# Last expert of a layer: the down product runs bank by bank, and the output rows of the first bank are taken during the second

## What is computed

```python
def expert_choice_ffn(h, w_router, w_gate, w_up, w_down):
    ...
    aff = jax.nn.softmax(jnp.dot(xs, w_router).astype(jnp.float32), axis=-1)
    cap = EC_FACTOR * n // N_EXPERTS
    gates, idx = lax.top_k(aff.T, cap)
    xe = xs[idx]
    hid = jax.nn.silu(jnp.einsum('ecd,edf->ecf', xe, w_gate)) * jnp.einsum('ecd,edf->ecf', xe, w_up)
    ye = jnp.einsum('ecf,efd->ecd', hid, w_down) * gates[..., None].astype(h.dtype)
    out = jnp.zeros_like(xs).at[idx.reshape(-1)].add(ye.reshape(-1, D))
```

## Time and profile before

| what | us |
|---|---|
| median of 3 runs | 1947.42 |
| lowest and highest run | 1946.61, 1949.61 |
| the profiled execution, its own time | 1943.12 |
| its span | 1941.4 |
| PE busy | 1824.8 (94%) |
| DVE busy | 651.0 (34%) |
| last `down` of layer 0, first to last start | 963.61 to 975.61 |
| last `down` of layer 1, first to last start | 1914.46 to 1926.72 |

### The profile page before, as it was taken

One profiled execution on the slowest core, in us unless ns is written; L12 is line 12 of the kernel. 1 busy time (PEld: TensorE's weight loads), 2 busy tenths in 40 slices (PEclk: granted clock), 3 DMA queues, 4 the chain that ended last, 5 costly groups with the idle time before them and its releaser, 6 DMA issues. The chain is left out here.

```text
span 1941.4 us, 34715 instructions
## 1 busy us (share of the span) xinstructions
PE 1824.8 (94%) x14950; PEld 871.9 (45%) x14950; DVE 651.0 (34%) x1394; ACT 378.1 (19%) x904; POOL 200.8 (10%) x275
## 2 busy tenths in 40 slices
PE   5999989959999999999999999999599999999996
PEld 2455655422434343434455566554233434343443
DVE  2345885350212121212243457833421212121211
ACT  2224653120101000000032256421110100000000
POOL 1004300000000000000010331000000000000000
PEclk8999999979999999999999999999799999999998
DMA  9750022237999999999995201131489999999993
GB/s 385 292 227 1 1 106 114 82 137 285 389 401 399 401 405 400 411 395 412 397 356 195 109 1 65 42 152 65 179 331 396 404 400 410 398 411 394 410 387 104
DMA packets 56202, 526.51 MB, mean 271 GB/s; under 512 B 12047, under 2 KB 13695, under 8 KB 26143
## 3 DMA queue, kind: packets, MB, share of 16 engines
q1 hardware_dynamic: 49134, 501.44, 64.0%
q0 software_dynamic: 6336, 21.63, 4.7%
q10 hardware_dynamic: 672, 2.62, 0.3%
HBM read 503.91 MB, written 24.38 MB: 272 GB/s over the span
## 5 line engine op out<-in xcount | busy, mean ns | idle before, releaser
L621 PE MATMUL PS<-arena,xe 128*32 128x512 f32 x6144 | 670.2, 596 | 3.8 <-DVE xe L1438 3.8
L621 PEld LDWEIGHTS PS<-arena,xe 128*32 128x32 f32 x6144 | 195.5, 110 | 455.4 <-issue 451.1
L1449 DVE TENSOR_TENSOR RA<-RA,PS 96x512 f32<-96x512 f32 (+2 forms) x96 | 63.2, 684 | 646.9 <-ACT RA L1141 644.1
L645 PE MATMUL PS<-arena,hdT 128*32 128x512 f32 x1536 | 267.2, 596 | 6.7 <-DMA arena<-w_exp 4.8
L647 PE MATMUL PS<-arena,hdT 128*32 128x256 f32 x1024 | 264.8, 381 | 0.0
L687 PE MATMUL PS<-arena,RB 128*128 128x512 f32 (+1 forms) x480 | 183.4, 530 | 0.0
L650 PE MATMUL PS<-arena,hdT 128*32 128x256 f32 x1536 | 156.5, 380 | 0.0
L651 PE MATMUL PS<-arena,hdT 128*32 128x256 f32 x512 | 152.9, 380 | 0.0
L1141 ACT ACTIVATE RA<-PS 96x512 f32<-96x512 f32 x32 | 19.0, 593 | 670.1 <-PE PS L621 670.1
L1029 PE MATMUL PS<-arena,RB 128*128 128x512 f32 x320 | 138.9, 593 | 0.0
L647 PEld LDWEIGHTS PS<-arena,hdT 128*32 128x32 f32 x1024 | 110.2, 110 | 27.4 <-issue 0.5
(11 more groups left out here) (293 smaller groups left out, 1813.3 us busy)
## 6 DMA issues: line engine op xcount, KB each, us to landing
arena<-w_exp SPq DMA_DIRECT2D x192, 2048.0 KB, 13.4
arena<-ada_rest SPq DMA_DIRECT2D x16, 2048.0 KB, 8.2
ada<-ada_first SPq DMA_DIRECT2D x8, 2048.0 KB, 23.3
arena<-w_in SPq DMA_DIRECT2D x4, 2048.0 KB, 10.8
arena<-w_out SPq DMA_DIRECT2D x2, 4096.0 KB, 13.5
arena<-w_in SPq DMA_DIRECT2D x4, 1536.0 KB, 23.8
RC<-x_res SPq DMA_DIRECT2D x2, 2560.0 KB, 10.7
x_res<-RC SPq DMA_DIRECT2D x10, 512.0 KB, 2.6
```

The costliest lines, as they stand in the source:

```text
L621: last = mm(PS[GRP * q:GRP * (q + 1), c * 512:(c + 1) * 512], xe[:, k, GRP * grp:GRP * (grp + 1)], w[:, col_, :], start=(k == 0), stop=(k ...
L645: mm(PS[GRP * q:GRP * (q + 1), 1536:2048], tok(q), w[:, 0:512], start=first, **flags)
L1449: V.tensor_tensor(h_, h_, up, ALU.mult).then_inc(hm_rdy.sem, 1)
```

## The change

`last_down(l)` takes the place of the last `down` of each layer. It makes two sweeps over the eight chunks. The first does all that writes bank 3 and raises a new semaphore, `dn_low`; the second does all that writes bank 4. The products are the same ones, in another order. The wait for the second half of the weights stands at chunk 4 of the first sweep. `dn_used` is raised in the second sweep. On DVE `last_rows_out(l)` takes the place of the last `rows_out`: it takes 512 columns and two of the three small pieces behind `dn_low`, and 256 columns and the third small piece behind `dn_used`.

```diff
--- before.py
+++ after.py
@@ -358,6 +358,7 @@
         dn_used = Signal("dn_used", 2 * EXP, primed=True)
         sg_rdy = Signal("sg_rdy", 3 * EXP)
         hm_rdy = Signal("hm_rdy", 3 * EXP)
+        dn_low = Signal("dn_low", 1)
         ht_ps = Signal("ht_ps", EXP)
         hd_rdy = Signal("hd_rdy", EXP)
         ys_rdy = Signal("ys_rdy", EXP, primed=True)
@@ -652,6 +653,32 @@
                     if k % 4 == 3:
                         last.then_inc(dn_used.sem, 1)
 
+            def last_down(l):
+
+                E = l * EXP + EXP - 1
+                pe.wait_ge(ys_rdy.sem, E + 1)
+                pe.wait_ge(hd_rdy.sem, E + 1)
+                for k in range(KD):
+                    if k % 4 == 0:
+                        pe.wait_ge(ew_in[4 + k // 4].sem, E * 16 + 16)
+                    w = down_weights(k)
+                    for q in range(3):
+                        mm(PS[GRP * q:GRP * (q + 1), 1536:2048], hdT[:, k, GRP * q:GRP * (q + 1)], w[:, 0:512],
+                           start=(k == 0), stop=(k == KD - 1), skip_group_check=True)
+                    for grp in range(2):
+                        last = mm(PS[96:P, 1536 + grp * REST:1536 + (grp + 1) * REST], hdT[:, k, GRP * grp:GRP * (grp + 1)], w[:, MAIN:D],
+                                  start=(k == 0 and grp == 0), stop=(k == KD - 1), skip_group_check=True)
+                last.then_inc(dn_low.sem, 1)
+                for k in range(KD):
+                    w = down_weights(k)
+                    for q in range(3):
+                        mm(PS[GRP * q:GRP * (q + 1), 2048:2304], hdT[:, k, GRP * q:GRP * (q + 1)], w[:, 512:MAIN],
+                           start=(k == 0), stop=(k == KD - 1), skip_group_check=True)
+                    last = mm(PS[96:P, 2048:2304], hdT[:, k, 2 * GRP:3 * GRP], w[:, MAIN:D],
+                              start=(k == 0), stop=(k == KD - 1), skip_group_check=True)
+                    if k % 4 == 3:
+                        last.then_inc(dn_used.sem, 1)
+
             pe.wait_ge(dve_consts, 4)
             pe.wait_ge(pool_consts, 5)
             for l in range(LAYERS):
@@ -1092,7 +1119,7 @@
                     vectors_turned(l + 1)
                     mm(PS[:, 1024:1024 + P], ones[:, :], upto[:, :], start=True, stop=True).then_inc(iota_ps.sem, 1)
                     first_modulation(l + 1, range(4))
-                down(l * EXP + EXP - 1)
+                last_down(l)
                 if l + 1 < LAYERS:
                     first_modulation(l + 1, range(4, KD))
                 pe.wait_ge(ys_rdy.sem, ys_rdy.at(l, EXP))
@@ -1477,6 +1504,24 @@
                                           ALU.add, ALU.is_equal)
                 ins.then_inc(oh_rdy.sem, 1)
 
+            def last_rows_out(l):
+
+                E = l * EXP + EXP - 1
+                dve.wait_ge(landed.sem, E + 1)
+                column(None, l, EXP - 1, 1, idx_s[:, :], None)
+                V.tensor_scalar(gcur[:, :].unsqueeze(2), gall[:, :, EXP - 1:EXP], 1.0, None, ALU.mult).then_inc(idxs_rdy.sem, 1)
+                dve.wait_ge(idxs_rdy.sem, E + 1)
+                dve.wait_ge(dn_low.sem, dn_low.at(l, 1))
+                V.scalar_tensor_tensor(ys[:, 0:512], PS[0:SLOT, 1536:2048], gcur[0:SLOT, 0:1], g2r[:, 0:512], ALU.mult, ALU.mult)
+                for g in range(2):
+                    o = 1536 + g * REST
+                    V.scalar_tensor_tensor(ys[GRP * g:GRP * (g + 1), MAIN:D], PS[PAD:P, o:o + REST], gcur[PAD:P, g:g + 1],
+                                           g2x[:, 0, :], ALU.mult, ALU.mult)
+                dve.wait_ge(dn_used.sem, 2 * E + 3)
+                V.scalar_tensor_tensor(ys[:, 512:MAIN], PS[0:SLOT, 2048:2048 + REST], gcur[0:SLOT, 0:1], g2r[:, 512:MAIN], ALU.mult, ALU.mult)
+                V.scalar_tensor_tensor(ys[CAP_L:SLOT, MAIN:D], PS[PAD:PAD + CAP_C, 2048:2048 + REST], gcur[PAD:PAD + CAP_C, 2:3],
+                                       g2x[0:CAP_C, 1, :], ALU.mult, ALU.mult).then_inc(ys_rdy.sem, 1)
+
             for sem in primes:
                 V.memset(hold[:, :], 0.0).then_inc(sem, 1)
                 dve.wait_ge(sem, 1)
@@ -1898,7 +1943,7 @@
                 if l + 1 < LAYERS:
                     vectors_in(l + 1)
                     last_slots(l)
-                rows_out(l, EXP - 1, l * EXP + EXP - 1)
+                last_rows_out(l)
 
 
         @block.gpsimd
```

## The result

The changed kernel took 1952.6 us (median of 22 runs, 1949.62 to 1955.99); the kernel before took 1949.45 us (median of 22 runs, 1943.04 to 1952.59). The ratio is 1.0025, with a 95% interval of 1.0018 to 1.0032: slower by 3.5 to 6.2 us, about 4.8. Forecast were +3.5 us and a time of 1950.9, with the larger chance on no measurable change. The change is slower, and by 0.25% at the middle of the interval, a little more than the bound of 0.2%; the lower end of the interval, 0.18%, lies just under that bound.

The account below looks back on a forecast made before the run. PE was taken to bound the kernel, except for late down weights at both layer ends. 1.7 + 1.7 - 1.5 + 1.6 = +3.5 us on the median 1947.4 gave 1950.9, range 1947.3 to 1954.0.

Parts of the forecast that it names:

- The mechanism, the moved work and its place: Last down products: work behind the late second half of weights grows from 5.16 to 6.88 us, +1.7 us per layer.
- DVE's gain: End of layer 1: fewer row pieces stand behind the product's end, 1.0 us in place of 2.51, -1.5 us.
- Layer 0's rows have slack: End of layer 0: PE's own queue ends 0.6 us after DVE's rows, so a shorter DVE tail gains nothing.
- The delay passes through layer 1: Layer 0's 1.7 us reaches the end, since PE in layer 1 waits for no weights from 1000 to 1912 us.
- The clock: End of layer 1: the pause grows to some 3.6 us, the granted clock falls to 0.50, +1.6 us.
- the second fall: Layer 0, clock fall behind the new 1.9 us pause: left out of the sum, up to 1.7 us more.
- rival 3: Clock falls at the ends of both layers: +5.2 us, 1952.6; chance 0.23.
- the forecast of one short fall: One clock fall, at the end of layer 1: +3.5 us in all; chance 0.37.
- Rival 4: Second sweep bound by PE's instruction supply: 4.7 us, +5.8 at most, 1952.1; chance 0.10.
- Rival 5: Weights not late at the layer ends, so only DVE's saving stays: -1.5 us, 1945.9; chance 0.08.

Follow-up runs that it names:

- experiment 5: Changed kernel with idle PE products before the wait for the weights' second half, two in layer 0, four in layer 1; ratio 1.0013 to the kernel before.
- experiment 6: PE as in the changed kernel, DVE's output rows as in the kernel before, all behind the product's end; ratio 1.0024 to the kernel before.
- experiment 7: Changed kernel with layer 1's last down weights loaded about 20 us earlier into used gate and up places; ratio 0.9988 to the kernel before.
- experiment 10: Changed kernel unaltered, run again for a second profiled execution; no total time or ratio given.
- experiment 1: Kernel before with the two sweeps and split rows only at the end of layer 1; ratio 1.001.
- experiment 3: Changed kernel with the weights' wait put back after chunks 0 to 3 in both banks, split kept; ratio 0.9992 to the kernel before.
- experiment 8: Kernel before, old order, with layer 1's last down weights loaded early; ratio 0.9979.
- experiment 9: Kernel before with early down weights, two sweeps and split rows in layer 1, layer 0 as before; ratio 0.998.
- experiment 2: Kernel before with the two sweeps and split rows only at the end of layer 0; ratio 1.001.
- the three best versions: Kernel before with early layer 1 weights; that plus layer 1's new order; that plus layer 0's modulation moved forward, mid-product wait, split rows: 0.9979, 0.998, 0.9981.

## Why the prediction was partly right, and where it failed

- **The mechanism, the moved work and its place: right.** 1.72 us at each end. S0 is 10.47 to 10.48 us in the four executions of the new order without a fall behind the restart (experiments 5, 6, 7 and 10), against 8.74 to 8.75 in five with the wait in the middle (the first profile, experiments 1, 3, 8 and 9): 1.72. In layer 1, T1 without a fall is 8.57 against 8.45, and it contains the saved 1.6.
- **DVE's gain: right.** -1.5 was said, -1.6 measured (3.48 to 1.87; 13.61 to 12.01; 1.62 in experiment 6). 80 x 256 took 0.48 us (said: 0.50), 512 columns 0.75.
- **Layer 0's rows have slack: right.** In experiment 6 S0 is the same with them late.
- **The delay passes through layer 1: not contradicted.** In the changed kernel PE's list of waits again has no expert weights between 1000 and 1921 us. No run here isolates it better than experiment 2 does, and its interval runs from 0.6 us under the kernel before to 4.5 us over it.
- **The clock: the failed step.** The prediction put it as "The loss lies between 0 and 1.7 us, by where the fall comes; I take 1.6" for layer 1 and nothing for layer 0. The error was the bound: I had taken the slow stretch of 3.4 us in the earlier trace rows for the largest one. The fall inside the pause of 3.7 to 4.8 us lasted 6.8 us in all four profiled executions with the new order and an unfilled pause, and cost 2.8, 2.7, 2.9 and 2.4 us (the changed kernel twice, experiments 1 and 6; the time at half clock behind the restart, by two). The trace of the kernel before held such a price, and the prediction left it aside: at the start of layer 1 the clock is at 0.50 from 992.2 to 999.0, which is 5.65 us of work at half the pace, or 2.8 us lost. Timeline, then windows, of the kernel before:

```profile
993.37 6.44 PE L595 MATMUL PS<-ident,arena 128*128 128x128 f32 x32 [1.84 <-DVE arena L1400]
```

```profile
992.00:993.00 1.00, 0.00 (x0) 0.00 (x0) 0.93 (x2) 1.00 (x4) 0.72 (x2) 0.59 1.07 459
...
998.00:999.00 1.00, 1.00 (x7) 1.00 (x6) 0.75 (x1) 0.21 (x1) 0.00 (x0) 0.50 0.99 417
```

In layer 0 the second fall, which I left out, came in two of five (1.5 us each). My condition for leaving it out did hold: where the first half of the product ran at half clock (experiments 7 and 10) the pause behind it was 0.89 and 1.24 us and no fall followed. But that is two of the five; in the other three the pause was 2.78 to 2.98 us, and two of them had the fall.

Set against this, the old wait in layer 1 has a fall in one of four (1.7 us; 0.4 on average). The mean over these few executions is 2.7 + 0.6 - 0.4 = 2.9 us, and with 1.72 + 1.72 - 1.6 = 1.84 us that makes 4.7 us, beside 4.8 measured. That these two agree so closely is luck, with an interval of 3.5 to 6.2.

A second count includes what a fall in the first half of a product costs. From the first product of the last `down` to the one-hot product layer 0 took 15.44 us on the mean of the six executions with the wait in the middle (the kernel before twice, experiments 1, 3, 8 and 9) and 17.54 on that of the five with the new order; from the first product to POOL's transfer layer 1 took 16.64 us (the kernel before twice, and experiment 2) and 18.88 (the changed kernel twice, and experiment 1). By this count the change costs 2.10 + 2.24 = 4.34 us. In total rival 3, with 5.2 us, is nearer than the forecast of one short fall, but its two short falls are not what happened either: in the profiled executions it was one long fall in layer 1 each time and a short one in layer 0 now and then. What the size of a fall is rests on windows of the trace and on experiment 5, which takes it away by filling the pause. How often it comes rests on four or five executions each, and is an estimate.

- **Rival 4, the supply of instructions: out.** Eight chunks of the second sweep take 3.46 us for 3.44. PE issued 64 products in this time, 54 ns each. By the 62 ns for each product of the Trainium skill ("TensorE: Matmul & The Clock Gate", section "Wait — 56ns, not 53.3ns?") the sweep would have taken 4.0 us; that page ties the figure to a decoder setting, and at 54 ns for each product the trace doesn't agree with it here.
- **Rival 5, the other side: right as a condition.** With the weights on time the change gains 1.6 us (experiments 7 and 8).

What stays open: whether the one-hot product's later start is worth its full 1.7 us at the end of the program, how often the clock falls at either end, and which of the three best versions is the fastest.

## What to carry to other kernels

When a product waits for its operands in parts, reordering it changes how much work stands behind the last part's landing. Count that work first: here a sweep by output bank put 6.88 us there in place of 5.16, which cost more than the 1.6 us of row work it covered; the same split with the wait left in the middle cost nothing. A longer pause of PE is dearer than its length, because the clock may fall within it and stay low for several microseconds of the work that follows; a fall has to be priced from the restart to the end of the slow stretch, and its size read from all the falls that the trace holds, not from the one at the nearest pause. And the better cure for a late load at a loop's end was a free place for it: the last iteration's weights could be loaded into buffers that nobody fills any more.

## What was not expected of the hardware

Around the two products a fall of the granted clock came in two lengths, 3.4 us and 6.8 us; in the long ones the clock had fallen 1.0 to 2.0 us before PE restarted, in the short ones 0.4 us before it at most, or behind it. In one execution of the unchanged kernel the same wait was 2.81 us in place of 1.90, and the clock fell behind it, so equal programs differ by 1.7 us there. The length of a pause does not decide by itself. In layer 0, pauses of 2.98 and 3.38 us (experiment 6), 3.23 us (experiment 8) and 3.51 us (experiment 5) were followed by no fall, while one of 2.78 us (experiment 2) was, and so was that of 3.46 us in experiment 7. In layer 1 the fall came in all four executions with a pause of 3.69 to 4.82 us, in one with 2.81 us, and in none with 1.90 to 2.25 us.
